# Feed-forward outputs of fourteen of the 22 inner tiles as seven block products for pairs of output tiles

## The reference, cut to what matters

```python
def swiglu(h, w_gate_up, w_down):
    g, u = jnp.split(h @ w_gate_up, 2, axis=-1)
    return (jax.nn.silu(g) * u) @ w_down
```

## Time and profile before

| | |
|---|---|
| median of 3 runs | 3153.88 us (3153.31 to 3154.04) |
| profiled execution | 3152.22 us |
| its span | 3150.9 us |
| TensorE busy | 3119.1 us, 99% of the span |
| VectorE, ScalarE, GpSimd busy | 59%, 47%, 50% |
| granted TensorE clock, mean | 0.997 of full speed |

### The profile page before, as it was taken

One profiled execution on the slowest core, in us unless ns is written; L12 is line 12 of the kernel. 1 busy time (PEld: TensorE's weight loads), 2 busy tenths in 40 slices (PEclk: granted clock), 3 DMA queues, 4 the chain that ended last, 5 costly groups with the idle time before them and its releaser, 6 DMA issues. The chain is left out here.

```text
span 3150.9 us, 47707 instructions
## 1 busy us (share of the span) xinstructions
PE 3119.1 (99%) x18912; PEld 2783.9 (88%) x18912; DVE 1874.8 (59%) x2519; ACT 1484.3 (47%) x2243; POOL 1589.0 (50%) x814
## 2 busy tenths in 40 slices
PE   9999999999999999999999999999999999999999
PEld 8999888899989998888999877888999788889998
DVE  7545467754665654577564577557645786475553
ACT  6434433543454444335453455545434575454443
POOL 5666533666656655434665533226656112256654
PEclk9999999999999999999999999999999999999999
DMA  4323322332223322322332232322323223323322
GB/s 153 117 94 108 119 78 75 108 118 97 108 94 108 112 104 94 112 81 83 118 108 95 89 94 81 121 92 104 120 94 108 89 95 125 104 94 114 108 103 72
DMA packets 93292, 322.28 MB, mean 102 GB/s; under 512 B 10512, under 2 KB 14992, under 8 KB 93072
## 3 DMA queue, kind: packets, MB, share of 16 engines
q1 hardware_dynamic: 87680, 312.07, 28.7%
q10 hardware_dynamic: 5392, 7.17, 0.7%
HBM read 316.05 MB, written 2.10 MB: 101 GB/s over the span
## 5 line engine op out<-in xcount | busy, mean ns | idle before, releaser
L2943 POOL TENSOR_TENSOR wlo<-raws,whi 128x1024 fp32r<-128x1024 f32 x417 | 1094.5, 2632 | 1084.6 <-ACT whi L1119 1084.3
L1119 ACT ACTIVATE whi<-raws 128x1024 fp32r<-128x1024 f32 x470 | 491.4, 1052 | 409.0 <-PE bank L427 318.1
L423 PE MATMUL bank<-f_hh,whi 128*128 128x512 f32 x904 | 353.5, 391 | 7.9 <-ACT whi L1119 7.9
L424 PE MATMUL bank<-f_hl,whi 128*128 128x512 f32 x904 | 353.2, 391 | 0.0
L2955 POOL TENSOR_TENSOR f_hl<-f_u,f_hh 128x512 fp32r<-128x512 f32 x132 | 177.6, 1345 | 162.3 <-ACT f_hh L1212 162.3
L423 PE MATMUL bank<-gxh,whi 128*128 128x512 f32 x584 | 230.5, 395 | 11.4 <-DVE gxl L2023 11.4
L561 PE MATMUL bank<-gxh,whi 128*128 128x256 f32 x944 | 236.8, 283 | 0.7 <-ACT f_c L1236 0.7
L2940 POOL TENSOR_TENSOR f_sl<-raws,f_sh 128x512 fp32r<-128x512 f32 x118 | 153.5, 1300 | 165.6 <-ACT f_sh L1229 165.4
L561 PE MATMUL bank<-f_th,whi 128*128 128x256 f32 x944 | 236.7, 283 | 0.0
L562 PE MATMUL bank<-f_tl,whi 128*128 128x256 f32 x944 | 236.7, 283 | 0.0
L562 PE MATMUL bank<-f_tl,f_sh 128*128 128x256 f32 x944 | 236.7, 283 | 0.0
(11 more groups left out here) (515 smaller groups left out, 7914.1 us busy)
## 6 DMA issues: line engine op xcount, KB each, us to landing
raws<-stream SPq DMA_DIRECT2D x588, 512.0 KB, 3.3
xa_mem<-memT ACTq DMA_DIRECT2D x2, 1024.0 KB, 6.4
m_dk<-decay ACTq DMA_DIRECT2D x2, 514.0 KB, 4.6
x<-xT ACTq DMA_DIRECT2D x4, 256.0 KB, 5.5
x<-xT SPq DMA_DIRECT2D x4, 256.0 KB, 6.9
outT<-x SPq DMA_DIRECT2D x2, 512.0 KB, 3.0
m_ct<-cos ACTq DMA_DIRECT2D x2, 256.0 KB, 2.7
m_sn<-sin ACTq DMA_DIRECT2D x2, 256.0 KB, 3.4
```

The costliest lines, as they stand in the source:

```text
L423: pe.matmul(out, seq(hi, k, P), h, start=first and k == 0, stop=False)
L424: pe.matmul(out, seq(hi, k, P), l, start=False, stop=False)
L1119: act.activation(M.whi[r][:, :], M.raw[r][:, :], ACT.Copy).then_inc(*S.tick("hi", u))
L2943: pool.tensor_tensor(M.wlo[r][:, :], M.raw[r][:, :], M.whi[r][:, :].bitcast(F32), ALU.subtract).then_inc(*S.tick("lo", u))
```

## The change

`F_PARTS` becomes (0, 8), (8, 14), (14, 22), `F_RUNS` (0, 9), (9, 15), (15, 22). The outputs of parts 0 and 1 are computed two output tiles at a time as seven block products, with inner tiles in pairs as the inner block dimension: 7 x 4 x 3 matmuls of 256 columns per pair of outputs in part 0, 7 x 3 x 3 in part 1. These "down" steps and the gate and up steps are one sequence (`SEQS`), and each step uses the same machinery of sums, low parts and snapshots. Part 2 stays plain.

The moving operand needs turned combinations of each pair of hidden tiles, as it did for the input: for each of hidden tiles 0 to 13 VectorE makes parts of 256 columns from `f_u` into `xsd` (`turn_hidden`, one for an even tile, three for an odd one), ScalarE writes the high part and GpSimd the low part, 1024 columns each, once per pair. Of even hidden tiles only the first half of the columns is kept. In a down step GpSimd adds two scaled snapshots to x (`part`), and VectorE adds the rest (`c22`, `second_row`, `first_row`). The gate is scaled in its bank in place of `f_a`; snapshots lie in `acc` and `sq`. The host packs the down weights of parts 0 and 1 in blocks (`tail_units`); units keep their size and count.

```diff
-F_PARTS = ((0, 6), (6, 14), (14, 22))
-F_RUNS = ((0, 7), (7, 15), (15, 22))
+F_PARTS = ((0, 8), (8, 14), (14, 22))
+F_RUNS = ((0, 9), (9, 15), (15, 22))
 PLAIN = (4, 2, 2, 2, 2, 2)
 BLOCKED = (0, 2, 4, 6, 1, 3, 5, 7)
-HIDDEN = 9
...
                 out.extend([("gate", f, m), ("up", f, m)])
-            out.extend(("down", f, c, m) for m in range(KD))
...
+def sevens(f):
+
+    out = []
+    for c in range(3):
+        out += [("tile", m) for m in range(max(F_RUNS[c][0], PLAIN[f]), F_RUNS[c][1])]
+        if c < 2:
+            out += [("down", c, j) for j in range(KD // 2)]
+    return out
+
+
+SEQS = [sevens(f) for f in range(6)]
+
+
+def rows(f, s):
+
+    item = SEQS[f][s]
+    if item[0] == "tile":
+        return U["up", f, item[1]], U["gate", f, item[1]]
+    return U["down", f, item[1], 2 * item[2]], U["down", f, item[1], 2 * item[2] + 1]
+
+
+def block_tiles(f, s):
+
+    item = SEQS[f][s]
+    return KD // 2 if item[0] == "tile" else (F_PARTS[item[1]][1] - F_PARTS[item[1]][0]) // 2
+
...
             self.stack = st
-            out = self.group(f"f{f}", [("hh", HIDDEN * SEQ, F32R), ("hl", HIDDEN * SEQ, F32R), ("th", KD * SEQ, F32R),
-                                       ("tl", KD * SEQ, F32R)])
+            out = self.group(f"f{f}", [(name, 4 * SEQ, F32R) for name in ("oddh", "oddl", "tur0h", "tur0l", "tur1h", "tur1l")])
+            out |= self.group(f"f{f}", [("own", SEQ, F32R), ("th", KD * SEQ, F32R), ("tl", KD * SEQ, F32R)])
             out |= self.group(f"f{f}", [(name + str(n), 3 * SEQ, F32R) for n in (1, 0) for name in ("sh", "sl")])
-            out |= self.group(f"f{f}", [("a", SEQ, F32), ("s", SEQ, F32), ("u", SEQ, F32),
-                                        ("c16", SEQ, F32), ("c5", HALF, F32)])
+            out |= self.group(f"f{f}", [("s", SEQ, F32), ("u", 2 * SEQ, F32)])
         self.stack = outer
         return out
...
+def both(t, cols):
+
+    return t.rearrange("p (n c) -> p n c", n=2)[:, :, 0:cols]
+
+
+def turned_tile(T, p):
+
+    e = p % 4
+    return seq(T[f"tur{e // 2}h"], e % 2, 2 * SEQ), seq(T[f"tur{e // 2}l"], e % 2, 2 * SEQ)
+
+
+def hidden_tile(M, T, m):
+
+    if m >= PAIRED:
+        k = m - PAIRED
+        name, k = ("odd", (k + 3) % 4) if k < 4 else ("tur0", k - 4)
+        return seq(T[name + "h"], k), seq(T[name + "l"], k)
+    if m % 2:
+        return seq(T["oddh"], m // 2 % 4), seq(T["oddl"], m // 2 % 4)
+    e = m // 2 % 5
+    if e == 0:
+        return of_half(T["own"], 0), of_half(T["own"], 1)
+    return of_half(M.gxh, 1, 2 * e - 2), of_half(M.gxl, 1, 2 * e - 2)
+
+
+def hidden_cols(m):
+
...
+        def operands(s):
+
+            item = SEQS[f][s]
+            if item[0] == "tile":
+                return {1: gx_part[1, 1], 2: gx_part[2, 1], 3: gx_part[2, 2], 5: turns[0], 7: turns[1], 6: turns[2], 4: turns[3]}
+            ps = pairs_of(item[1])
+            even, odd = ([hidden_tile(M, T, 2 * p + n) for p in ps] for n in range(2))
+            out = {n: [tuple(t[:, at * HALF:(at + 1) * HALF] for t in turned_tile(T, p)) for p in ps]
+                   for at, n in enumerate((5, 7, 6, 4))}
+            out |= {1: even, 2: [(h[:, 0:HALF], l[:, 0:HALF]) for h, l in odd], 3: [(h[:, HALF:], l[:, HALF:]) for h, l in odd]}
+            return out
+
+        def pairs_of(c):
+            return range(F_PARTS[c][0] // 2, F_PARTS[c][1] // 2)
+
+        def fourth(s):
+
+            x, u = bank[BANK["x7", f, s]], rows(f, s)[1]
+            pe.wait_ge(*S.at("hi", u))
+            pe.wait_ge(*S.at("c22", f, s))
+            product(4, s, (seq(T[f"sh{s % 2}"], 0), seq(T[f"sl{s % 2}"], 0)), low_part(u), x[:, 0:HALF], False)
+
+        def seven(s):
+            item, (u1, u2) = SEQS[f][s], rows(f, s)
+            first, second, up_lo = u1 % SLOTS, u2 % SLOTS, low_part(u1)
+            sh, sl = T[f"sh{s % 2}"], T[f"sl{s % 2}"]
+            arrive = {}
+            if item[0] == "tile":
+                x_read, y_read = ("silu", f, item[1]), ("t", f, item[1])
+                if s == 0:
+                    arrive[5] = [("turned_lo", f, k) for k in range(4)]
+            else:
+                x_read, y_read = ("part_sum", f, item[1], 2 * item[2] + 1), ("part_sum", f, item[1], 2 * item[2])
+                if item[2] == 0:
+                    ps = pairs_of(item[1])
+                    arrive = {1: [("hidden", f, 2 * p) for p in ps], 5: [("turned_h_lo", f, p) for p in ps],
+                              2: [("hidden", f, 2 * p + 1) for p in ps]}
+            x = next_bank(*x_read)
+            pe.wait_ge(*S.at("hi", u1))
+            product(1, s, (seq(M.whi[first], 0), seq(M.wlo[first], 0)), up_lo, x[:, 0:HALF], True, arrive.get(1))
+            y = next_bank(*y_read)
+            pe.wait_ge(*S.at("s13_hi", f, s))
+            product(5, s, (seq(M.whi[second], 0), seq(M.wlo[second], 0)), ("s13_lo", f, s), y[:, HALF:], True, arrive.get(5))
+            if s:
+                fourth(s - 1)
+            pe.wait_ge(*S.at("s24_hi", f, s))
+            pe.wait_ge(*S.at("snap1", f, s))
+            product(6, s, (seq(sh, 1), seq(sl, 1)), ("s24_lo", f, s), x[:, 0:HALF], False)
+            pe.wait_ge(*S.at("snap5", f, s))
+            product(2, s, (seq(M.whi[first], 1), seq(M.wlo[first], 1)), up_lo, y[:, 0:HALF], False, arrive.get(2))
+            product(3, s, (seq(sh, 2), seq(sl, 2)), ("s24_lo", f, s), y[:, HALF:], False)
+            pe.wait_ge(*S.at("snap6", f, s))
+            product(7, s, (seq(M.whi[second], 1), seq(M.wlo[second], 1)), ("s13_lo", f, s), x[:, 0:HALF], False)
 
         if f == 0:
-            a, b = next_bank("a", 0, 0), next_bank("t", 0, 0)
+            a, b = next_bank("silu", 0, 0), next_bank("t", 0, 0)
             high(("gate", 0, 0), a[:, :], [("gx", i - 1, k) for k in range(KD)])
             high(("up", 0, 0), b[:, :])
             low(("gate", 0, 0), a[:, :])
...
-        for c in range(2):
-            run(c)
-            pairs, arrive = hidden(c)
-            for m in range(KD):
-                unit(("down", f, c, m), next_bank("part_sum", f, c, m)[:, :], pairs, arrive=arrive if m == 0 else None)
-                if m == 0:
-                    fourth(F_RUNS[c][1] - 1)
-        run(2)
-        pairs, arrive = hidden(2)
...
+        def snap(n, s):
+
+            item = SEQS[f][s]
+            src = bank[BANK["y7", f, s]][:, HALF:] if n == 5 else bank[BANK["x7", f, s]][:, 0:HALF]
+            out = M.acc[:, 0:HALF] if n == 5 else of_half(M.sq, n // 6)
+            scale = 1.0 if item[0] == "tile" else -F_SCALE[f] if n == 5 else F_SCALE[f]
+            act.wait_ge(*S.at("seven", f, s, n))
+            if s:
+                before = SEQS[f][s - 1]
+                if before[0] == "tile":
+                    act.wait_ge(*S.at("c22" if n == 5 else "c1", f, s - 1))
                 else:
-                    split_hi(U["down", f, c, 1])
-                snap(5, m, y[:, HALF:], T["c5"][:, :], "c22")
-                if more:
-                    s24_hi(m + 1)
-                    m22_hi(m + 1)
-                if m > first or c == 0:
-                    silu(m - 1)
-                snap(6, m, x[:, 0:HALF], T["c16"][:, HALF:], "c1")
-                if m > first or c == 0:
-                    hidden_hi(m - 1)
+                    act.wait_ge(*S.at("part_pool", f, before[1], 2 * before[2] + (n == 5)))
+            act.activation(out, src, ACT.Copy, scale=scale).then_inc(*S.tick(f"snap{n}", f, s))
+
+        def step(s):
+            after = s + 1 if s + 1 < len(SEQS[f]) else None
+            before = SEQS[f][s - 1] if s else ("tile", PLAIN[f] - 1)
+            split_hi(U["down", f, 2, 0] if after is None else rows(f, after)[0])
+            snap(1, s)
+            if after is None:
+                split_hi(U["down", f, 2, 1])
+            else:
+                s13_hi(after)
+            snap(5, s)
+            if after is not None:
+                s24_hi(after)
+                m22_hi(after)
+            if before[0] == "tile":
+                silu(before[1])
+            snap(6, s)
+            if before[0] == "tile":
+                hidden_hi(before[1])
 
         def tile(m):
             ahead(("gate", f, m))
...
+        def c22(s):
+            item, x = SEQS[f][s], at_bank("x7", f, s)
+            dve.wait_ge(*S.at("seven", f, s, 7))
+            if item[0] == "tile":
+                dve.wait_ge(*S.at("snap5", f, s))
+                dve.tensor_tensor(x[:, HALF:], x[:, 0:HALF], M.acc[:, 0:HALF], ALU.add).then_inc(*S.tick("c22", f, s))
+                return
+            m = 2 * item[2] + 1
+            out = of_half(M.x, 1, m)
+            dve.wait_ge(*S.at("part_pool", f, item[1], m))
+            dve.scalar_tensor_tensor(out, x[:, 0:HALF], -F_SCALE[f], out, ALU.mult, ALU.add).then_inc(*S.tick("c22", f, s))
+
+        def second_row(s):
+            _, c, j = SEQS[f][s]
+            m = 2 * j + 1
+            out = of_half(M.x, 0, m)
+            dve.wait_ge(*S.at("seven", f, s, 4))
+            if c:
```

(120 more changed lines are left out.)

326 lines of the change are left out of this document (130 added, 196 removed).

## The result

The changed kernel takes **3321.56 us** (median of four runs, 3320.16 to 3322.18) against 3153.60 us for the kernel before on the same chip (3152.16 to 3154.04): a ratio of 1.0535, with a 95% interval of 1.0522 to 1.0548, so 5.35% slower. The profiled execution has a span of 3320.0 us. Forecast were 3326 us, between 3225 and 3392.

The account below looks back on a forecast made before the run. TensorE bounds the kernel before, with the helpers' 10.05 us round 0.03 under it. Less 34.0 us of gain, 207.4 us of waits add 173 to 3152.2, forecast 3326 us, range 3225 to 3392.

Parts of the forecast that it names:

- The gain: Down parts 0 and 1: fewer, shorter matmuls save 5.7 us per FFN, 34 us over six.
- The rounds: Helper engines' loop per gate/up tile: 12.65 us odd, 9.46 even; a pair takes 22.1 against TensorE's 20.16.
- What limits the tile steps: Tile steps: product 2 waits for snapshot 5, ready at h+7.4 (odd) or h+5.4 (even), h being f_u's start.
- The start: Block steps' start, tiles 0 and 1: VectorE's sum behind GpSimd's wlo delays snapshot 5; waits of 4.7 us.
- The walk through the second FFN: Waits added stretch by stretch through the second FFN: 34.9 us per FFN, 32.9 in the first, 207.4 in all.
- start, tiles 2 to 7, first boundary: Second FFN: 4.7 at the start, 5.8 for three pairs, 3.9 for product 5's turned tile 7; together 14.4 us.
- rest of part 0: Down steps of part 0: helper round 10.5 us against TensorE's 10.08; waits of 2.6 us.
- tiles 9 to 14, second boundary: Second FFN: two pairs, less slack, 2.25 us, then 5.8 at the boundary for product 5; 8.1 in the sum.
- down steps of part 1: Helper round 9.5 us against TensorE's 7.56; waits of 9.8 us, including 1.5 at tile 15.
- Faster: Whole kernel: only the two boundaries per FFN wait, 23 us in all; 3141 us, chance 0.08.
- Lower throttling: VectorE's last turn gets the port before GpSimd, odd round 11.8 us; 3228 to 3269 us, chance 0.24.
- More throttling: Even tiles: GpSimd's wlo goes ahead of VectorE's sum, round 11.8 us, a pair loses 4.2; 3391 us, chance 0.13.

Follow-up runs that it names:

- experiment 1: Changed kernel with the four turning operations of VectorE reading one operand from PSUM in tiles done as block products (wrong values): 3280.4 us.
- Experiments 4: Changed kernel without turned tiles (wrong outputs) and with down steps combined in PSUM by VectorE, without GpSimd's adds to x: 3136.7 us.
- experiment 9: Kernel before with one wait per FFN, TensorE waiting for five GpSimd fills ahead of part 1's sixth down unit: 3183.3 us against 3155.3.
- experiments 5 to 7: Changed kernel with R multiplied by VectorE: 3254.2 us; also down steps combined in PSUM: 3205.4; also boundary pair's turned low part by VectorE, high part first: 3180.3.
- experiment 8: Changed kernel with down steps in PSUM, R and boundary low part by VectorE, plus GpSimd's low parts waiting for VectorE's first sum: 3137.1 us.
- numbers 3: Changed kernel with down steps combined in PSUM by VectorE and added to x there, without GpSimd's two adds: 3256.5 us.

## Why the prediction was right, step by step

**The gain:** 34.0 us forecast, 34.4 in the trace. Right.

**The rounds:** odd 12.65 forecast, 12.30 measured; even 9.46 and 9.44. The cause was the one named, the last turn behind GpSimd's subtraction; experiment 1 took it away and the turn was 0.42 us. Over by 0.35: the odd round lost less to the port than I added up, the turned low part ends at h+7.3, not h+7.65.

**What limits the tile steps: amount right, place of the wait wrong.** I put the limit at snapshot 5 and product 2, and named waits of 1 to 2 us ahead of product 2 as the sign. The waits that show, 18 of 0.7 to 0.8 us behind odd tiles, are for c22 ahead of product 4. TensorE, and then ScalarE's snapshot 5, in the odd round that begins at 645.55:

```profile
649.65 0.36 PE L616 MATMUL bank<-f_th,f_sh 128*128 128x256 f32 x1 [0.75 <-DVE bank L2183]
...
652.75 0.39 PE L616 MATMUL bank<-gxh,whi 128*128 128x256 f32 x1
...
652.33 0.38 ACT L1323 ACTIVATE acc<-bank 128x256 f32<-128x256 f32 x1
```

c22 stands behind the three turns on VectorE's queue, and product 4 comes ahead of product 2, so most of the delay is spent there; I had passed over it. Yet snapshot 5 ends at 652.71, and product 2 starts at 652.75. The snapshot's chain (VectorE's sums, ScalarE's whi) does not go through product 4, so without the wait for c22 product 2 would have stood until then all the same. The limit was the one named, h+7.2 in place of h+7.4.

**The start:** 4.7 us in every FFN forecast (by the times given the first part is 594.4 - 591.27 = 3.1, not 3.3). In the first two there is none above 1.2; in the last four it is 2.7 to 3.7, for snapshot 5. Timelines of VectorE and GpSimd at the start, second FFN and fourth:

```profile
616.35 1.22 DVE L2157 TENSOR_TENSOR banks<-raws 128x1024 f32<-128x1024 f32 x1
...
1573.16 2.99 DVE L2157 TENSOR_TENSOR banks<-raws 128x1024 f32<-128x1024 f32 x1
...
616.86 2.97 POOL L3065 TENSOR_TENSOR wlo<-raws,whi 128x1024 fp32r<-128x1024 f32 x1 [0.97 <-ACT whi L1188]
...
1572.66 2.41 POOL L3065 TENSOR_TENSOR wlo<-raws,whi 128x1024 fp32r<-128x1024 f32 x1
```

In the second FFN the sum is issued 0.51 us ahead of wlo and takes 1.22; in the fourth it is 0.50 behind and takes 2.99. The sum comes equally late in both, 3.1 us behind f_u. It is wlo that moved: in the second FFN it waited 0.97 us for ScalarE's whi. The forecast had the order of the fourth for all six; it holds in the last four.

**The walk through the second FFN,** waits without half clock:

| | forecast | measured |
|---|---|---|
| start, tiles 2 to 7, first boundary | 14.4 | 0.9 + 3.6 + 5.0 = 9.5 |
| rest of part 0 | 2.6 | 2.1 |
| tiles 9 to 14, second boundary | 8.1 | 1.3 + 4.8 = 6.1 |
| down steps of part 1 | 9.8 | 7.3 |
| sum | 34.9 | 25.0 |

The stretches and their order are right, every sum is too high by a fifth to a third. The first boundary alone was under: 5.0 where I had 3.9, since less of the delay had been used up before it. The second was over, 4.8 where I had 5.8; the working that gives 3.85 at the first gives 7.65 - 1.56 - 1.64 = 4.45 there, and the prediction does not show where the rest comes from. In part 0 the adds to x come 10.27 us apart (10.5 forecast), in part 1 9.4 to 10.2 (9.5).

**The missing term:** half clock. 207 us of waits were forecast, 164 came, and 44 us of half clock stood in for the rest. So the total was right to 0.13% by luck, by two errors that cancel. (The last step is off too: 3325.6 plus the 1.7 us named there is 3327, not 3326.) Without the clock the sum would have come out near 3279, still inside the range. Experiments 4 and 9 show that the clock follows the waits. This step of the prediction failed: it put the clock's cost at nothing, without a reason. The stretches that it read have almost no wait in the kernel before and no half clock. But the same trace has waits elsewhere, five of 2.2 to 2.5 us and one of 5.8 us, and the granted clock is 0.5 beside two of the five and for 6.8 us at the long one. With waits of 4 to 5 us in the forecast, that was to be priced.

**The rivals.** Faster was excluded by the rounds, as argued: two of the helpers' rounds take 21.74 us against TensorE's 20.16. Lower throttling wanted VectorE's last turn ahead of GpSimd; it was behind, 1.50 us long, though the waits, 164, lie nearer to its 151 than to the forecast 207. TensorE's busy share is 95%, where the prediction had 93. More throttling, wlo ahead of the sum in even rounds, didn't happen in the changed kernel, where in every even round between the start and a boundary the sum takes 1.22 us, but did in experiments 5 to 7.

**What stays open:** the share of each part in experiment 8. It stands on numbers 3, 5 and 7; the added wait alone on the changed kernel was not tried. Nor is it shown what decides whether a wait of 2 to 3 us brings half clock; one of the six of experiment 9, that of the first FFN, did not.
